# The last stage of a mixture-of-experts decoder step: a buffer for every tile, all gathers at once, no barrier, residuals put in PSUM ahead

## The chip, the cores and the metric

One core of a Trainium2 chip runs the whole step as one program. The metric is the device time of one execution in microseconds (us), lower is better. The core's engines each run their own instruction list: TensorE (PE in the rows, with PEld for its weight loads), VectorE (DVE), ScalarE (ACT), GpSimd (POOL) and SyncE (SP). They meet only at semaphores. Data moves between memory and the on-chip buffers by DMA, which SP, ACT and POOL issue.

## The reference

One step of a one-layer decoder: attention and a recurrent mixer, then a hierarchical mixture of experts, for 1024 prompt tokens and 32 sample tokens, all in float32. What matters here is the end of it:

```python
x = x + mixed @ w_out[l]                          # x1 in the kernel
for e in range(N_EXPERTS):
    he = jax.nn.silu(t @ w1[e]) * (t @ w3[e])
    y = y + combine[:, e:e + 1] * (he @ w2[e])
x = x + y                                         # two experts a token have combine > 0
y_prompt = rmsnorm(xp, final_norm_w)
```

Each token has two chosen experts with gates `gate1` and `gate2`. So the last stage computes, for a token, x1 + gate1 * ya + gate2 * yb, where ya and yb are the two experts' outputs for it, and then the root mean square norm of that row times `final_norm_w`.

## The kernel before

The kernel sorts the (token, expert) pairs by expert. An expert loop runs over blocks of 160 sorted rows, two blocks a turn (`s` = 0 and 1, `turns` + 1 turns). For a block TensorE flips the rows (L1947, L1949), computes the hidden layer (L1962) and the down projection (L1977 for 32 rows, L1982 for 128), ACT and DVE copy the halves of the result out of PSUM (L1910, L1912, L2057), and ACT stores them to `ye_d`, the expert scratch in memory (L1914, L1916). The last block's store is the last thing that the last stage needs, since a token's rows can be in any block.

The last stage runs over TILES = 9 tiles of tokens: eight of 128 rows and one of 32. `x1[i]` holds the residual rows of tile i on chip. `phase_end` (L450 to 453) is a barrier: each engine drains, increments one semaphore and waits until all five have. Behind it, for tile i:

- POOL gathers the two experts' rows from `ye_d` into `ya` and `yb` (L1895, one indirect DMA each). There are YBUF = 5 pairs of buffers. From tile 5 on POOL first waits for ACT's sum of squares of tile i - 5 and for the output store of that tile.
- TensorE puts the residual into two PSUM banks by a product with the identity (L2005; banks 2 * (i % 4) and the next, and from tile 4 on it waits for the combination of tile i - 4, by `x2_ready`), waits for the gather of `yb`, and adds the product of diag(gate2) with `yb` into the same banks (L2008). Each of these two is a group of two matmuls of 512 columns, each of which the rows count as two instructions, so x4. Below they are called the residual and the gated product.
- DVE combines, ya * gate1 + PSUM, in two halves (L2085, `combine`), and later takes the inverse root of tile i's mean square by five small instructions (L2019 and L2025 to L2028, `mean_eps` and `inverse`) and scales the row with `fw` (L2097, the result). Its order is combine(0), then for each i: combine(i + 1), the inverse root of i, the result of i.
- ACT sums the squares (L1931) and takes their root (L1934); ahead of the tiles it loads `fw` (L1927).
- SP stores the result (L1865).

The semaphore `mixed` tells DVE that a gated product is done, `x2_ready` tells ACT and TensorE that a combination is done, `ssf` and `rmsf` are ACT's, `y_ready` lets SP store. Every engine executes its list in order, and there is no planner: the order of the work is the order in which the lines stand.

Of the kernel before, what the change touches and what calls it, by code (L numbers as in the profile page):

```python
# [10 lines left out]
ALU = mybir.AluOpType  # L11
# [4 lines left out]
P = 128  # L16
D = 1024
# [107 lines left out]
def build(nc, x_prompt, x_sample, cache_k, cache_v, state_hgrn, page_table,  # L125
# [30 lines left out]
    with ExitStack() as ctx:  # L156
# [89 lines left out]
        YBUF = 5  # L246
        ya = [take(D, T0 + i * D) for i in range(YBUF)]
        yb = [take(D, T0 + (YBUF + i) * D) for i in range(YBUF)]
        fw = take(D, T0 + 2 * YBUF * D)
        diag2 = take(TILES * P, G0 + 64)  # L250

        tab = sb("tab", SMALL)
# [1594 lines left out]
        @block.sync  # L1847
        def _(sp):
            turns = sp.value_load(more_i[0:1, 0:1], min_val=1, max_val=PAIRS - 1)
            with sp.Fori(0, turns) as t:  # L1850
                for s in range(2):
                    e = sp.value_load(eid[0:1, ds(t * 2 + (s + 2), 1)], min_val=0, max_val=NE - 1)
                    w13 = wslot[s][:, 0:4096].rearrange("p (k f) -> p k f", k=KC)
                    sp.wait_ge(sem("h1_ps"), t * 2 + s + 1)
                    sp.dma_start(w13[:, :, 0:FF], w1_v[ds(e * D, D), :].rearrange("(k p) f -> p k f", p=P)).then_inc(sem(f"wexp{s}"), 16)
                    sp.wait_ge(sem("h_ps"), t * 2 + s + 3)
                    sp.dma_start(w13[:, :, FF:2 * FF], w3_v[ds(e * D, D), :].rearrange("(k p) f -> p k f", p=P)).then_inc(sem(f"wthr{s}"), 16)
                    sp.wait_ge(sem("ye_ps"), t * 6 + 3 * s + 9)
# [7 lines left out]
            for i in range(YBUF):  # L1866
                sp.wait_ge(sem(f"y_out{i}"), 16 * len(range(i, TILES, YBUF)))

        @block.gpsimd
        def _(pool):  # L1870
# [13 lines left out]
            with pool.Fori(0, turns) as t:  # L1884
                for s in range(2):
                    pool.wait_ge(sem("xgT_ps"), t * 2 + s + 1)
                    gather(t + 1, s)
            phase_end(pool, 1)

            for i in range(TILES):  # L1890
                if i >= YBUF:
                    pool.wait_ge(sem("ssf"), i - YBUF + 1)
                    pool.wait_ge(sem(f"y_out{i % YBUF}"), 16 * (i // YBUF))
                for c, buf in enumerate((ya, yb)):
                    pool.indirect_dma_start(out=buf[i % YBUF][0:ROWS[i], :], out_offset=None, in_=ye_d,  # L1895
                                            in_offset=bass.IndirectOffsetOnAxis(ap=slot_i[0:ROWS[i], c * TILES + i:c * TILES + i + 1], axis=0)).then_inc(sem(f"yg{c}{i % YBUF}"), 16)

        @block.scalar
        def _(act):
# [22 lines left out]
                    results(t, s)  # L1922
            act.wait_ge(sem("ye_out0"), nit * 32 + 32)
            act.wait_ge(sem("ye_out1"), nit * 32 + 32)
            act.sem_inc(sem("ye_seen"), 1)
            phase_end(act, 1)
            act.dma_start(fw, final_norm_w.rearrange("(a n) -> a n", a=1).broadcast_to([P, D])).then_inc(sem("fw"), 16)  # L1927
            for i in range(TILES):
                r = ROWS[i]
                act.wait_ge(sem("x2_ready"), i + 1)  # L1930
                nc.scalar.activation(yb[i % YBUF][0:r, :], ya[i % YBUF][0:r, :], ACT.Square,  # L1931
                                     accum_out=ss[0:r, i:i + 1]).then_inc(sem("ssf"), 1)
                act.wait_ge(sem("ssf"), i + 1)
                nc.scalar.activation(rstd[0:r, i:i + 1], ss[0:r, i:i + 1], ACT.Sqrt, scale=1.0 / D, bias=epsc[0:r, :]).then_inc(sem("rmsf"), 1)  # L1934

        @block.tensor
        def _(pe):
# [57 lines left out]
            with pe.Fori(0, turns) as t:  # L1995
                pair(t, True)
            pair(turns, False)
            phase_end(pe, 1)

            for i in range(TILES):  # L2000
                r = ROWS[i]
                if i >= 4:
                    pe.wait_ge(sem("x2_ready"), i - 3)
                for n in range(2):
                    nc.tensor.matmul(ps[2 * (i % 4) + n][0:r, :], ident[0:r, 0:r], x1[i][0:r, n * 512:(n + 1) * 512], start=True, stop=False)  # L2005
                pe.wait_ge(sem(f"yg1{i % YBUF}"), 16 * (i // YBUF + 1))
                for n in range(2):
                    mm = nc.tensor.matmul(ps[2 * (i % 4) + n][0:r, :], diag2[0:r, i * P:i * P + r], yb[i % YBUF][0:r, n * 512:(n + 1) * 512], start=False, stop=True)  # L2008
                mm.then_inc(sem("mixed"), 1)

        @block.vector
        def _(dve):
# [62 lines left out]
            dve.wait_ge(sem("fw"), 16)  # L2075

            ch2 = Chain(dve, sem("dve_last"))

            def combine(i):
                r = ROWS[i]  # L2080
                dve.wait_ge(sem(f"yg0{i % YBUF}"), 16 * (i // YBUF + 1))
                dve.wait_ge(sem("mixed"), i + 1)
                a_ = ya[i % YBUF][0:r, :]
                for n in range(2):
                    last = V.scalar_tensor_tensor(out=a_[:, n * 512:(n + 1) * 512], in0=a_[:, n * 512:(n + 1) * 512], scalar=gate1[0:r, i:i + 1],  # L2085
                                                  in1=ps[2 * (i % 4) + n][0:r, :], op0=ALU.mult, op1=ALU.add)
                last.then_inc(sem("x2_ready"), 1)

            combine(0)
            for i in range(TILES):  # L2090
                if i + 1 < TILES:
                    combine(i + 1)
                r = ROWS[i]
                dve.wait_ge(sem("rmsf"), i + 1)
                ch2.step(mean_eps(ss[0:r, i:i + 1], D))
                inverse(rstd[0:r, i:i + 1], ss[0:r, i:i + 1], ch2)
                V.scalar_tensor_tensor(out=ya[i % YBUF][0:r, :], in0=ya[i % YBUF][0:r, :], scalar=rstd[0:r, i:i + 1], in1=fw[0:r, :],  # L2097
                                       op0=ALU.mult, op1=ALU.mult).then_inc(sem("y_ready"), 1)


# [29 lines left out]
```

## Time and profile before

| | |
|---|---|
| three runs, median | 1472.09 us (1469.22 to 1472.66) |
| the profiled execution | 1467.2 us, span 1465.4 us |
| its mean granted TensorE clock | 0.94 of full speed |
| TensorE, DVE, ACT, POOL busy | 87%, 43%, 25%, 8% of the span |
| from the first gather to the end of the span | 1414.37 to 1465.4, 51 us |

The span is the profiled execution's time from its first to its last recorded event; the 1.8 us around it are start and end of the program. Times in rows are microseconds from the span's start.

### The profile page before, as it was taken

Reading aid. Unit: us, or ns where it says so; the run is one execution under the profiler, and the core shown is the slowest. Engines: PE = TensorE matmul, PEld = TensorE weight load, DVE = VectorE, ACT = ScalarE, POOL = GpSimd, SP = SyncE. Lnnn points to the kernel's source line nnn. Section 1 sums busy time; section 2 is a strip of 40 time slices with the busy share of each in tenths; the row PEclk is TensorE's granted clock in tenths of the full one; section 3 lists DMA queues with packets and bytes.
Section 4 is the critical chain, followed back from the end, with each engine's and each line's share of the span. In section 5 each row is a group of like instructions: output and inputs, shape, how many; then the busy total and the mean of one; then the engine's idle time right before and its main releaser. Section 6 shows DMA issues by size and latency. Waiting matters only on the chain. (4 is left out here: it accounts for less than half of the span.)

```text
span 1465.4 us, 24091 instructions
## 1 busy us (share of the span) xinstructions
PE 1268.1 (87%) x9162; PEld 894.7 (61%) x9162; DVE 633.4 (43%) x1518; ACT 372.8 (25%) x748; POOL 111.2 (8%) x272
## 2 busy tenths in 40 slices
PE   0899998989999899988787886999995299999976
PEld 0566785767678788655364553555553188888842
DVE  0401314445354646366866764467336212121117
ACT  3401200121212224244545552222212011111113
POOL 0500000000000001020000000000000111111022
PEclk9999998999999999999898988999997599999999
DMA  7521101010020106667786969999840679999746
GB/s 207 205 111 51 58 29 43 30 31 30 0 88 1 60 3 215 229 249 260 287 299 237 318 231 380 334 355 348 299 152 19 208 250 304 297 304 299 251 174 231
DMA packets 163717, 274.02 MB, mean 187 GB/s; under 512 B 19041, under 2 KB 78178, under 8 KB 163618
## 3 DMA queue, kind: packets, MB, share of 16 engines
q1 hardware_dynamic: 141072, 221.90, 44.6%
q0 software_dynamic: 11104, 38.28, 7.3%
q10 hardware_dynamic: 11442, 12.51, 2.7%
q8 instruction: 63, 1.03, 0.3%
q14 instruction: 36, 0.29, 0.1%
HBM read 235.55 MB, written 37.09 MB: 186 GB/s over the span
## 5 line engine op out<-in xcount | busy, mean ns | idle before, releaser
L973 PE MATMUL bank<-arena 128*128 128x352 f32 x768 | 237.6, 468 | 0.0
L973 PEld LDWEIGHTS bank<-arena 128*128 128x128 f32 x768 | 146.8, 194 | 80.2 <-issue 5.2
L976 PE MATMUL bank<-arena 128*128 128x256 f32 (+1 forms) x864 | 195.2, 383 | 0.6 <-issue 0.6
L976 PEld LDWEIGHTS bank<-arena 128*128 128x128 f32 (+1 forms) x864 | 155.0, 182 | 33.0 <-issue 5.7
L1546 DVE STREAM_TRANSPOSE arena<-arena 128x512 f32<-128x512 f32 x256 | 156.2, 677 | 21.4 <-DMA arena<-in_cache_k_dram 21.0
L1962 PEld LDWEIGHTS bank<-arena 128*128 128x128 f32 x1024 | 142.6, 192 | 9.2 <-issue 9.2
L1962 PE MATMUL bank<-arena 128*128 128x160 f32 x1024 | 143.7, 302 | 1.9 <-DVE arena L2047 1.9
L1250 PE MATMUL bank<-arena 128*128 128x512 f32 x256 | 119.7, 611 | 7.5 <-DMA arena<-in_w_out_dram 7.5
L1095 PE MATMUL bank<-arena,tab 128*32 128x256 f32 x1024 | 71.3, 426 | 19.8 <-ACT arena L779 13.1
L1250 PEld LDWEIGHTS bank<-arena 128*128 128x128 f32 x256 | 46.9, 193 | 60.8 <-issue 53.0
L719 ACT ACTIVATE arena<-bank 128x352 f32<-128x352 f32 x48 | 22.2, 463 | 224.5 <-PE bank L973 224.5
L1095 PEld LDWEIGHTS bank<-arena,tab 128*32 128x32 f32 x1024 | 33.7, 120 | 58.5 <-issue 27.3
L1136 PE MATMUL bank<-arena 128*32 128x128 f32 x2048 | 65.9, 275 | 0.1
L851 ACT ACTIVATE arena<-arena,small 128x128 f32<-128x128 f32 (+7 forms) x64 | 48.9, 765 | 63.5 <-DVE small L1610 63.5
L2052 DVE TENSOR_TENSOR arena<-arena,bank 128x320 f32<-128x320 f32 x16 | 7.8, 488 | 130.4 <-PE bank L1962 130.4
L1180 PE MATMUL bank<-arena 64*128 64x512 f32 (+3 forms) x192 | 58.7, 618 | 6.1 <-DVE small L1610 6.0
L1136 PEld LDWEIGHTS bank<-arena 128*32 128x32 f32 x2048 | 53.0, 110 | 16.5 <-issue 14.7
L1982 PE MATMUL bank<-arena 128*128 128x512 f32 x128 | 59.2, 605 | 0.0
L1016 PEld LDWEIGHTS bank<-arena 128*128 128x128 f32 x448 | 54.3, 192 | 4.4 <-issue 0.4
L1016 PE MATMUL bank<-arena 128*128 128x128 f32 x448 | 54.6, 275 | 0.0
L1472 DVE COPY_PREDICATED arena<-tab,bank 128x512 f32<-128x512 int32 x56 | 37.4, 721 | 36.0 <-PE bank L1020 36.0
L1202 PE MATMUL bank<-arena 128*128 128x128 f32 x288 | 46.5, 303 | 7.0 <-ACT arena L872 7.0
(306 smaller groups left out, 1474.6 us busy)
## 6 DMA issues: line engine op xcount, KB each, us to landing
arena<-in_cache_k_dram SPq DMA_DIRECT2D x256, 256.0 KB, 4.7
arena<-in_cache_v_dram SPq DMA_DIRECT2D x256, 256.0 KB, 3.9
arena<-in_expert_w_dram SPq DMA_DIRECT2D x48, 1024.0 KB, 8.6
arena<-in_w_in_dram SPq DMA_DIRECT2D x14, 1024.0 KB, 5.1
expert_scratch<-route POOLq DMA_DIRECT2D x40, 256.0 KB, 5.6
expert_scratch<-arena ACTq DMA_DIRECT2D x16, 512.0 KB
out_dram<-arena SPq DMA_DIRECT2D x12, 512.0 KB, 2.9
arena<-in_x_prompt_dram SPq DMA_DIRECT2D x4, 1024.0 KB, 10.9
```

Of the source, the lines that this page charges most:

```text
L851: nc.scalar.activation(zp[n % 2][:, sl], zp[n % 2][:, sl], ACT.Exp, scale=-1.0, bias=a[:, m:m + 1], accum_out=a[:, 2 + m:3 + m]).then_inc( ...
L973: mm = nc.tensor.matmul(bank(g)[:, 0:N3], w[:, k, c * P:(c + 1) * P], hT[:, k * TOK + n * N3:k * TOK + (n + 1) * N3], start=(k == 0), stop ...
L976: mm = nc.tensor.matmul(bank(g)[0:ROWS[c], 0:256], tok(hT, k, c), w[:, k, :], start=(k == 0), stop=(k == KC - 1))
L1016: mm = nc.tensor.matmul(ps[bb + c // 4][:, (c % 4) * P:(c % 4 + 1) * P], a, b_, start=True, stop=True)
L1095: mm = nc.tensor.matmul(ps[5][32 * h:32 * h + 32, 0:256], q[:, c * 32:(c + 1) * 32], k8[:, :, c, :], start=(j == 0), stop=(j == 3))
L1136: mm = nc.tensor.matmul(ps[7][32 * h:32 * h + 32, 0:P], lhs, ring4[q4 % QUADS][:, i * HW + h * P:i * HW + (h + 1) * P], start=(g == 0 and ...
L1180: nc.tensor.matmul(ps[k % 3][:, 0:w], qT[rows, h * TOK + i * P:h * TOK + (i + 1) * P], kT[rows, h * TOK + j * P:h * TOK + j * P + w], star ...
L1202: mm = nc.tensor.matmul(ps[4][:, 0:P], pT[k % PCH][:, (jj % 4) * P:(jj % 4 + 1) * P], v_nat[:, jj * HW + h * P:jj * HW + (h + 1) * P], sta ...
L1250: mm = nc.tensor.matmul(ps[n][:, :], tok(mix_da if kk < H else mix_hg, kk % H, i), wout[k][:, n * 512:(n + 1) * 512], start=(k == 0), stop ...
L1546: V.transpose(page, page).then_inc(sem("k_flip"), 1)
L1962: mm = nc.tensor.matmul(ps[3 + m // 2][:, (m % 2) * TR:(m % 2 + 1) * TR], w13[:, k, m * P:(m + 1) * P], xT[s][:, k * TR:(k + 1) * TR], sta ...
L1982: mm = nc.tensor.matmul(ps[5 + n][:, :], he[s][:, k * TR:k * TR + P], w2[:, k * D + n * 512:k * D + (n + 1) * 512], start=(k == 0), stop=( ...
```

## The change

`ya` and `yb` get nine buffers each; `yb` takes over the space of the experts' weights, `ya` and `fw` that of the expert loop's blocks. With that all waits of POOL inside the last stage go, and it issues its 18 gathers in one go, each pair counted on one semaphore for tile i. All five calls of `phase_end` go; POOL waits for the stores' own semaphores instead. TensorE puts the residuals of tiles 0 to 3 into the eight banks as soon as the expert loop has left them, and inside the loop over tiles the residual of tile i + 4 stands behind the gated product of tile i. ACT computes one Sqrt ahead of the tiles on a value that isn't used, and then takes one Sqrt for two tiles. DVE takes the inverse root for two tiles at a time, in an order with the results two tiles behind the combinations.

```diff
@@ sync
-            phase_end(sp, 1)
             for i in range(TILES):
                 sp.wait_ge(sem("y_ready"), i + 1)
                 dst = ys_v if i == TILES - 1 else yp_v[:, i, :]
-                sp.dma_start(dst, ya[i % YBUF][0:ROWS[i], :]).then_inc(sem(f"y_out{i % YBUF}"), 16)
+                sp.dma_start(dst, ya[i][0:ROWS[i], :]).then_inc(sem("y_out"), 16)
...
@@ gpsimd
-            phase_end(pool, 1)
-
+            pool.wait_ge(sem("ye_out0"), turns * 32 + 64)
+            pool.wait_ge(sem("ye_out1"), turns * 32 + 64)
+            pool.sem_inc(sem("ye_seen"), 1)
             for i in range(TILES):
-                if i >= YBUF:
-                    pool.wait_ge(sem("ssf"), i - YBUF + 1)
-                    pool.wait_ge(sem(f"y_out{i % YBUF}"), 16 * (i // YBUF))
                 for c, buf in enumerate((ya, yb)):
...
@@ scalar
-            act.sem_inc(sem("ye_seen"), 1)
-            phase_end(act, 1)
             act.dma_start(fw, final_norm_w.rearrange("(a n) -> a n", a=1).broadcast_to([P, D])).then_inc(sem("fw"), 16)
+            nc.scalar.activation(att[:, 0:1], epsc, ACT.Sqrt)
             for i in range(TILES):
                 r = ROWS[i]
                 act.wait_ge(sem("x2_ready"), i + 1)
...
+                nc.scalar.activation(yb[i][0:r, :], ya[i][0:r, :], ACT.Square, accum_out=ss[0:r, i:i + 1]).then_inc(sem("ssf"), 1)
+                if i % 2 or i == TILES - 1:
+                    j = i - i % 2
+                    act.wait_ge(sem("ssf"), i + 1)
+                    nc.scalar.activation(rstd[0:r, j:i + 1], ss[0:r, j:i + 1], ACT.Sqrt, scale=1.0 / D, bias=epsc[0:r, :]).then_inc(sem("rmsf"), 1)
@@ tensor
-            phase_end(pe, 1)
-
+            def residual(i):
+                r = ROWS[i]
+                for n in range(2):
+                    nc.tensor.matmul(ps[2 * (i % 4) + n][0:r, :], ident[0:r, 0:r], x1[i][0:r, n * 512:(n + 1) * 512], start=True, stop=False)
+
+            pe.wait_ge(sem("xT_s"), turns * 6 + 9)
+            residual(0)
+            pe.wait_ge(sem("ye_a"), turns * 4 + 6)
+            pe.wait_ge(sem("ye_v"), turns * 2 + 3)
+            residual(1)
+            residual(2)
+            residual(3)
             for i in range(TILES):
                 r = ROWS[i]
-                if i >= 4:
-                    pe.wait_ge(sem("x2_ready"), i - 3)
+                pe.wait_ge(sem(f"yg{i}"), 32)
                 for n in range(2):
-                    nc.tensor.matmul(ps[2 * (i % 4) + n][0:r, :], ident[0:r, 0:r], x1[i][0:r, n * 512:(n + 1) * 512], start=True, stop=False)
-                pe.wait_ge(sem(f"yg1{i % YBUF}"), 16 * (i // YBUF + 1))
-                for n in range(2):
-                    mm = nc.tensor.matmul(ps[2 * (i % 4) + n][0:r, :], diag2[0:r, i * P:i * P + r], yb[i % YBUF][0:r, n * 512:(n + 1) * 512], start=False, stop=True)
+                    mm = nc.tensor.matmul(ps[2 * (i % 4) + n][0:r, :], diag2[0:r, i * P:i * P + r], yb[i][0:r, n * 512:(n + 1) * 512], start=False, stop=True)
                 mm.then_inc(sem("mixed"), 1)
+                if i + 4 < TILES:
+                    pe.wait_ge(sem("x2_ready"), i + 1)
+                    residual(i + 4)
@@ vector
-            phase_end(dve, 1)
...
+            def scales(i):
+                r, j = ROWS[i], i - i % 2
+                dve.wait_ge(sem("rmsf"), j // 2 + 1)
+                ch2.step(mean_eps(ss[0:r, j:i + 1], D))
+                inverse(rstd[0:r, j:i + 1], ss[0:r, j:i + 1], ch2)
...
+            dve.wait_ge(sem("fw"), 16)
             combine(0)
...
+            combine(1)
+            for i in range(2, TILES):
+                combine(i)
+                if i % 2 == 0:
+                    scales(i - 1)
+                result(i - 2)
+            result(TILES - 2)
+            scales(TILES - 1)
+            result(TILES - 1)
```

## Rows read from the trace of the kernel before

**Rows 1.** Page, part 1: engine, busy us, share of the span, instructions.
```profile
PE 1268.1 (87%) x9162; PEld 894.7 (61%) x9162; DVE 633.4 (43%) x1518; ACT 372.8 (25%) x748; POOL 111.2 (8%) x272
```

**Rows 2.** Timeline, 1404 to 1416 us: start, duration, engine, line; idle time before, releaser.
```profile
1404.55 0.49 DVE L2052 TENSOR_TENSOR arena<-arena,bank 128x320 f32<-128x320 f32 x1 [7.91 <-PE bank L1962]
...
1405.28 1.07 PE L1977 MATMUL bank<-arena 128*32 128x256 f32 x16 [0.76 <-DVE arena L2052]
...
1406.28 3.70 PE L1982 MATMUL bank<-arena 128*128 128x512 f32 x8
...
1410.87 0.35 ACTq L1916 DMA_DIRECT2D expert_scratch<-arena  x1
...
1414.37 0.94 POOL L1895 DMA_INDIRECT arena<-expert_scratch,route  x1 [49.49 <-ACTq L452]
...
1415.61 0.94 POOL L1895 DMA_INDIRECT arena<-expert_scratch,route  x1 [0.31 <-issue]
```

**Rows 3.** Chain that ended last, two pieces: start, us, what.
```profile
1410.87 3.12 DMA expert_scratch<-arena
...
1415.61 6.00 DMA arena<-expert_scratch,route
```

**Rows 4.** Timeline, tiles 0 to 3, 1421 to 1436 us.
```profile
1421.65 3.44 PE L2008 MATMUL bank<-arena 128*128 128x512 f32 x4 [3.92 <-DMA arena<-expert_scratch,route]
...
1425.24 1.41 DVE L2085 SCALAR_TENSOR_TENSOR arena<-arena,route,bank 128x512 f32<-128x512 f32 x2 [14.54 <-PE bank L2008]
...
1426.65 1.88 PE L2008 MATMUL bank<-arena 128*128 128x512 f32 x4
...
1426.68 1.06 ACT L1931 ACTIVATE arena<-arena 128x1024 f32<-128x1024 f32 x1 [17.79 <-DVE arena L2085]
...
1427.85 1.28 ACT L1934 ACT_TABLE_LOAD   x1
...
1428.64 1.41 DVE L2085 SCALAR_TENSOR_TENSOR arena<-arena,route,bank 128x512 f32<-128x512 f32 x2 [1.99 <-PE bank L2008]
...
1432.08 1.41 DVE L2085 SCALAR_TENSOR_TENSOR arena<-arena,route,bank 128x512 f32<-128x512 f32 x2
...
1434.24 1.28 DVE L2097 SCALAR_TENSOR_TENSOR arena<-arena,small 128x1024 f32<-128x1024 f32 x1
```

**Rows 5.** Timeline, TensorE at tiles 5 and 6, 1442 to 1450 us.
```profile
1442.68 1.98 PE L2008 MATMUL bank<-arena 128*128 128x512 f32 x4 [2.13 <-DMA arena<-expert_scratch,route]
...
1444.50 1.88 PE L2005 MATMUL bank<-arena,tab 128*128 128x512 f32 x4
...
1448.04 1.98 PE L2008 MATMUL bank<-arena 128*128 128x512 f32 x4 [1.66 <-DMA arena<-expert_scratch,route]
```

**Rows 6.** Waits, 1400 to 1466 us: total us, times, longest.
```profile
DVE arena L2085 <- PE bank L2008: 21.2, 5, 14.5
POOL arena L1895 <- DMA out_dram<-arena: 17.1, 4, 9.1
```

**Rows 7.** Timeline, tile 8's combination and the last result.
```profile
1457.48 1.39 DVE L2085 SCALAR_TENSOR_TENSOR arena<-arena,route,bank 32x512 f32<-32x512 f32 x2
...
1461.61 1.27 DVE L2097 SCALAR_TENSOR_TENSOR arena<-arena,small 32x1024 f32<-32x1024 f32 x1
```

**Rows 8.** The gathers' line, L1895: time from issue to landing.
```profile
DMA to landing us min/median/max: 6.0/6.7/7.8
```

**Rows 9.** DMA queues, 1380 to 1466 us: POOL's queue, packets, MB, share.
```profile
q0 software_dynamic: 2400, 8.65, 27.4%
```

**Rows 10.** Windows: length; busy PE, PEld, DVE, ACT, POOL; granted clock, DMA share, GB/s.
```profile
650.00:651.00 1.00, 1.00 (x4) 0.55 (x4) 0.34 (x2) 0.97 (x4) 0.77 (x4) 0.50 1.01 406
...
1422.00:1423.00 1.00, 1.00 (x2) 0.48 (x2) 0.00 (x0) 0.00 (x0) 0.76 (x1) 0.50 1.02 414
...
1441.00:1442.00 1.00, 0.00 (x0) 0.00 (x0) 0.96 (x2) 0.83 (x3) 0.18 (x1) 1.00 1.04 426
```

**Rows 11.** Timeline, TensorE around 649 us.
```profile
649.50 0.33 PE L1192 MATMUL bank<-tab,arena 128*128 128x128 f32 x1 [1.05 <-DVE arena L1622]
```

More of the change, by code:

```diff
@@ L244, in build @@
         ysb, ysm = [take(D, M0[s] + 2624) for s in range(2)], [take(256, M0[s] + 3648) for s in range(2)]
[L246 to L249, printed above, removed]
+        ya = [take(D, T0 + i * D) for i in range(TILES)]
+        yb = [take(D, C0 + i * D) for i in range(TILES)]
+        fw = take(D, T0 + TILES * D)
         diag2 = take(TILES * P, G0 + 64)
@@ L1864, in _ @@
                 dst = ys_v if i == TILES - 1 else yp_v[:, i, :]
-                sp.dma_start(dst, ya[i % YBUF][0:ROWS[i], :]).then_inc(sem(f"y_out{i % YBUF}"), 16)
-            for i in range(YBUF):
-                sp.wait_ge(sem(f"y_out{i}"), 16 * len(range(i, TILES, YBUF)))
+                sp.dma_start(dst, ya[i][0:ROWS[i], :]).then_inc(sem("y_out"), 16)
+            sp.wait_ge(sem("y_out"), 16 * TILES)
         @block.gpsimd
@@ L1887, in _ @@
                     gather(t + 1, s)
-            phase_end(pool, 1)
+            pool.wait_ge(sem("ye_out0"), turns * 32 + 64)
+            pool.wait_ge(sem("ye_out1"), turns * 32 + 64)
+            pool.sem_inc(sem("ye_seen"), 1)
             for i in range(TILES):
-                if i >= YBUF:
-                    pool.wait_ge(sem("ssf"), i - YBUF + 1)
-                    pool.wait_ge(sem(f"y_out{i % YBUF}"), 16 * (i // YBUF))
                 for c, buf in enumerate((ya, yb)):
-                    pool.indirect_dma_start(out=buf[i % YBUF][0:ROWS[i], :], out_offset=None, in_=ye_d,
-                                            in_offset=bass.IndirectOffsetOnAxis(ap=slot_i[0:ROWS[i], c * TILES + i:c * TILES + i + 1], axis=0)).then_inc(sem(f"yg{c}{i % YBUF}"), 16)
+                    pool.indirect_dma_start(out=buf[i][0:ROWS[i], :], out_offset=None, in_=ye_d,
+                                            in_offset=bass.IndirectOffsetOnAxis(ap=slot_i[0:ROWS[i], c * TILES + i:c * TILES + i + 1], axis=0)).then_inc(sem(f"yg{i}"), 16)
         @block.scalar
@@ L1930, in _ @@
                 act.wait_ge(sem("x2_ready"), i + 1)
[L1931 to L1934, printed above, removed]
+                nc.scalar.activation(yb[i][0:r, :], ya[i][0:r, :], ACT.Square, accum_out=ss[0:r, i:i + 1]).then_inc(sem("ssf"), 1)
[3 more added lines that the diff above has]
+                    nc.scalar.activation(rstd[0:r, j:i + 1], ss[0:r, j:i + 1], ACT.Sqrt, scale=1.0 / D, bias=epsc[0:r, :]).then_inc(sem("rmsf"), 1)
         @block.tensor
@@ L2071, in _ @@
             pair(turns, False)
-            phase_end(dve, 1)
-            dve.wait_ge(sem("fw"), 16)
             ch2 = Chain(dve, sem("dve_last"))
@@ L2080, in combine, with result @@
                 r = ROWS[i]
-                dve.wait_ge(sem(f"yg0{i % YBUF}"), 16 * (i // YBUF + 1))
                 dve.wait_ge(sem("mixed"), i + 1)
-                a_ = ya[i % YBUF][0:r, :]
                 for n in range(2):
-                    last = V.scalar_tensor_tensor(out=a_[:, n * 512:(n + 1) * 512], in0=a_[:, n * 512:(n + 1) * 512], scalar=gate1[0:r, i:i + 1],
+                    last = V.scalar_tensor_tensor(out=ya[i][0:r, n * 512:(n + 1) * 512], in0=ya[i][0:r, n * 512:(n + 1) * 512], scalar=gate1[0:r, i:i + 1],
                                                   in1=ps[2 * (i % 4) + n][0:r, :], op0=ALU.mult, op1=ALU.add)
                 last.then_inc(sem("x2_ready"), 1)
-            combine(0)
[L2090 to L2098, printed above, removed]
+            def scales(i):
[3 more added lines that the diff above has]
+                inverse(rstd[0:r, j:i + 1], ss[0:r, j:i + 1], ch2)
+            def result(i):
+                r = ROWS[i]
+                V.scalar_tensor_tensor(out=ya[i][0:r, :], in0=ya[i][0:r, :], scalar=rstd[0:r, i:i + 1], in1=fw[0:r, :],
+                                       op0=ALU.mult, op1=ALU.mult).then_inc(sem("y_ready"), 1)
+            dve.wait_ge(sem("fw"), 16)
+            combine(0)
+            combine(1)
[7 more added lines that the diff above has]
+            result(TILES - 1)
 _INS = ['x_prompt', 'x_sample', 'cache_k', 'cache_v', 'state_hgrn', 'page_table', 'norm1_w', 'w_in', 'rel_bias',
```

## The prediction

> **What bounds the kernel now.** The page comes first: TensorE is busy 87% of the span [rows 1]. That average is made by the stages ahead; the change touches only what comes after the last expert, so I read the timeline and the chain from 1405 us on. There the last down-projection ends at 1409.98, and ACT's store of its result is issued at 1410.87 and lands at 1413.99. Only then can a row be gathered: POOL's first gather starts at 1414.37, tile 0's second at 1415.61. That one takes 6.0 us to land, and TensorE starts tile 0's gated product at 1421.65 [rows 2 to 4]. The last stage proper is thus 1421.65 to 1465.4, 43.8 us.
>
> Inside it each tile needs 1.72 us of TensorE for the residual product and 1.72 for the gated one (TensorE works there without a gap, two groups every 3.43 us; a single group's own span, with its drain, is 1.88), and on DVE 1.41 for the combination, about 0.75 for the inverse root (from the end of the combination, 1433.49, to the result's start at 1434.24) and 1.27 for the result. Both sums are 3.43 to 3.44 us, and combinations do follow each other so: 1428.64, 1432.08 [rows 4]. So in its free running part TensorE and DVE are equal bounds, because the residual of tile i+1 runs while DVE combines tile i. From tile 5 on the gathers come late: POOL waits 17.1 us in four waits for output stores that free its five buffers, and TensorE starts tiles 5 and 6 late, after pauses of 2.13 and 1.66 us [rows 5, 6]. DVE's five waits are 21.2 us, of which 14.5 lie ahead of tile 0 and 1.99 ahead of tile 1 [rows 4, 6]. The other three make 4.7 us: that is all that the buffers cost at the end of the path. After tile 8's combination (1457.48 + 1.39) the results of tiles 7 and 8 end at 1462.88, and the end of the span, 1465.4, is 2.5 us later [rows 7].
>
> **The change, part by part.**
>
> *Barrier.* The first gather starts 0.38 us after the store landed (1413.99 to 1414.37). POOL also needs 0.31 between two gathers without any barrier [rows 2, 3]. So the removal is worth 0 to 0.4 us; I take 0.1, since a wait, a semaphore and the same preparation stay ahead of the gather.
>
> *Buffers and gathers.* 18 gathers at 1.24 us each [rows 2] start from 1414.3 to 1435.4 and, with landings of 6.0 to 7.8 us [rows 8], are in by 1443.2. The bytes don't forbid it: 8.65 MB for the gathers and 0.5 MB for the norm weights, at the 414 GB/s of a busy stretch, take 22 us; an output store of 0.5 MB adds 1.3 us [rows 9, 10]. The pairs are ready well before the times that I find below, so no gather is late any more: the 4.7 us go. Late next is then whatever orders TensorE and DVE.
>
> *Residuals ahead.* Four residual groups run on TensorE from 1410 to about 1417 (four times 1.72), in time in which it waits anyway [rows 2, 4]. In the kernel before, tile 0's residual hid behind its gather too, and the others beside DVE. Gain 0 as long as DVE keeps up; what follows from their order is more. But all eight banks are then full, and tile i+4's residual needs the banks of tile i. TensorE works in program order, and the new order is: gated product i, wait for the combination of i, residual i+4, gated product i+1. Behind the new wait stands the gated product of the next tile, though its rows have landed and its banks are ready; DVE waits for that. What were two engines side by side becomes one loop:
> gated product's start to DVE's start 1.99 (1426.65 to 1428.64, DVE idle before) + combination 1.41 + DVE's end to TensorE's start 0.24 (1405.04 to 1405.28) + residual after a wait until the next group 1.82 (1442.68 to 1444.50) = 5.46 us a tile [rows 2, 4, 5]. The hand-over from DVE is the least sure term. From below it can be DVE's to ACT, 0.03 (1426.65 to 1426.68), which makes 5.25; above it, I keep 0.3, for 5.5. I take 0.24, which is the same pair of engines.
> The Trainium skill, "TensorE: Matmul & The Clock Gate", section Step-by-step: what each phase is for, says that only weight loads are pulled ahead and matmuls stay in program order. No row here shows a matmul overtaking one that waits. If one could, the loop would not exist, and the sum would be that of the first rival.
>
> *The sum.* Tile 0's combination starts at 1425.24 - 0.1 = 1425.14. Residuals 4 to 8 follow combinations 0 to 4, so the loop runs five times: tile 5's combination starts at 1425.14 + 5 x 5.46 = 1452.44. DVE keeps up meanwhile: its longest work between two combinations is 0.75 + 1.27 = 2.02, and it has 5.46 - 1.41 = 4.05. From there on no residual is left (tiles 6 to 8 follow at 1.72) and DVE is the bound. Its list from the combination of 5 on is 4 combinations, 6 results (3 to 8) and 3 inverse roots (for 4-5, 6-7, 8): 5.64 + 7.62 + 2.25 = 15.5 us. The last result ends at 1467.95; with the same 2.5 us of store and end [rows 7] the span is 1470.5 against 1465.4: +5.1 us.
>
> *Where that stands against the kernel before.* The loop costs 5 x (5.46 - 3.43) = 10.1. DVE's lists from tile 0 on differ by four inverse roots (3.0 saved), but most of the saving falls into DVE's idle time inside the loop. The results are kept back by one tile more, so after the last combination there stand an extra result (1.27), while 4.7 of stalls are gone.
>
> *Small parts.* ACT's table load (1.28 us, at 1427.85) moves ahead of tile 0 into idle time; before, it ended at 1429.13, covered by the combination of tile 1 until 1430.05 [rows 4]; without that cover it would have cost its 1.28 once. Gain 0. Sums of squares (1.06 + 0.19) and half as many Sqrts lie beside DVE work; one pair follows 1.6 us after its combination, while DVE has a combination or result to do: 0, at most 1.27 if DVE were out of work. SP's stores have no queue ahead of them.
>
> **Against the runs.** The profiled run took 1467.2 us, 1.8 over its span; the runs' median, 1472.09, is 4.9 above it. The change is in the last 50 us, so I add the difference to both: 1472.3 in the form of that profiled run, and 1477.2 us against the median.
>
> **The rivals.**
>
> *No loop: DVE alone is the bound.* If residual i+4 didn't hold back the gated product (say, because the next group was let through), DVE would run through: 9 x 1.41 + 9 x 1.27 + 5 x 0.75 = 27.9 from 1425.14, end 1453.0 + 2.5 = 1455.5, so -9.9 us: 1462.2. For it: DVE's waits would be gone with the late gathers. Against it: the order of the waits in the code, and TensorE's program order. Its point of decision is whether DVE's work between two combinations exceeds 4.05 us; it is 2.02.
>
> *The first group runs at the full clock.* The clock is a second term in tile 0. TensorE had paused 3.9 us before 1421.65 and its gated product took 3.44 us at granted clock 0.50 (the 1.2 GHz level); the same group at 1426.65 took 1.88 at 2.4 GHz, and the pauses of 2.13 and 1.66 us later did not lower the clock [rows 4, 5, 10]. After the change the pause is about 4.6 us (1417 to 1421.6), so I expect the same low start. If it stays high instead, 3.44 becomes 1.88 and all moves 1.6 us earlier: +3.5, 1475.6, which counts as no change.
>
> *The loop lowers the clock.* This is the side beyond the forecast. In the loop TensorE works 3.7 us and pauses 1.76. Rows for: at 649.50 it had paused 1.05 us amid smaller products, and in the microsecond from 650 on the clock was 0.50 [rows 10, 11]. Rows against: with pauses of that size and the very same products the groups at 1442.68 and 1448.04 took 1.98, full clock [rows 5, 10]. One stretch of low clock costs about what it cost for tile 0, 1.6 us; two of them make +8.3, 1480.4; if it stayed low, each of ten groups would cost 1.56 more, +20.7, 1493.
> The Trainium skill's page on TensorE, section A second HAM failure mode: psum-queue depth-cycling, describes just this: short idle times between groups that cycle through banks make the clock swing. By it this rival would be the rule; the trace of this stage doesn't show it, so it keeps a small chance.
>
> *The change does little.* If the order were right but the hand-overs shorter (5.25 a tile), the sum is +4.0; with a store or landing saved at the end it drops to +2 or 3: no change by measurement.
>
> **How the numbers follow.** A measurement of this kernel can tell about 0.3% (4.4 us) from no change. Chances: forecast loop at full clock 0.55, with its own range +3.4 to +6.5 (1475.5 to 1478.6), of which I put 0.13 under 4.4 us; low clock in the loop 0.15; full clock at the first group 0.12; little change by shorter terms 0.08; no loop, faster 0.10. So faster 0.10, same 0.33, slower 0.57. The likeliest is the forecast, 1477.2. For the range I leave out the fast rival (0.10) and the far end of the low clock: 1471.5 to 1484, which also takes in a couple of microseconds by which medians of such runs differ (1469.2 to 1472.7 before).
>
> **What would show it.** Right: combinations of tiles 0 to 5 start some 5.4 us apart, DVE and TensorE both idle inside each; TensorE's residual waits for DVE's combination line; all gathers start 1.24 us apart and none is waited for after tile 0; from tile 5 on DVE has no idle time for 15.5 us. Wrong: combinations 3 us apart from the start (no loop), a granted clock of 0.5 after 1428, or gathers that land more than 20 us after their start.

## The result, and the profile after

The median of 22 runs after is 1476.51 us (lowest 1471.89, highest 1481.06) against 1470.64 us (1464.51 to 1477.19) of 22 runs of the kernel before beside it. The ratio is 1.0039 with a 95% interval of 1.0028 to 1.0050: slower by 5.9 us, where +5.1 was forecast. The profiled execution took 1474.43 us, span 1472.6, which is 7.2 us above the span before; the forecast span was 1470.5.

The page's engine line answers [rows 1]; nothing can be read from it alone, the change lies in 50 us of 1470.

```profile
PE 1269.7 (86%) x9162; PEld 894.1 (61%) x9162; DVE 630.1 (43%) x1498; ACT 371.7 (25%) x745; POOL 111.3 (8%) x272
```

The chain that ended last, from the last expert's store on (start, us, what), answers [rows 3]:

```profile
1410.96 3.13 DMA expert_scratch<-arena
1414.12 0.79 issue
1414.91 0.94 POOL arena L1890
1415.85 0.30 issue
1416.16 5.40 DMA arena<-expert_scratch,route
1421.56 0.04 issue
1421.60 3.80 PE bank L2009 x4
1425.44 0.06 issue
1425.50 1.42 DVE arena L2082 x2
1426.92 0.04 issue
1426.96 3.78 PE bank L1996 x4
1430.74 1.90 PE bank L2009 x4
1432.67 1.42 DVE arena L2082 x2
1434.09 0.04 issue
1434.13 1.98 PE bank L1996 x4
1436.12 1.73 PE bank L2009 x4
1437.87 1.42 DVE arena L2082 x2
...
1449.73 1.97 PE bank L1996 x4
1451.70 3.51 PE bank L2009 x4
1455.23 1.40 DVE arena L2082 x2
```

L2082 is the combination, L1996 the residual product, L2009 the gated one. The chain is the predicted loop: combination, residual, gated product, combination, with TensorE waiting for each combination and each combination for TensorE. Combinations start at 1425.50, 1432.67, 1437.87, 1443.07, 1448.27 and 1455.23: three steps of 5.20 us, and one of 7.17 and one of 6.96 at the ends.

The timeline of TensorE over the same stretch (start, duration, line, idle time before and its releaser) answers [rows 4, 5]. It shows both what was expected, the pauses of 1.5 us for DVE, and what wasn't: the residual at 1426.96 takes 3.78, and the gated product after the small residual of tile 8 (32 rows) is slow too: 3.51 in the chain above. The last row puts it together with the three products behind it.

```profile
1421.60 3.78 PE L2009 MATMUL bank<-arena 128*128 128x512 f32 x4 [4.67 <-DMA arena<-expert_scratch,route]
1426.96 3.78 PE L1996 MATMUL bank<-arena,tab 128*128 128x512 f32 x4 [1.58 <-DVE arena L2082]
1430.54 2.10 PE L2009 MATMUL bank<-arena 128*128 128x512 f32 x4
1434.13 1.98 PE L1996 MATMUL bank<-arena,tab 128*128 128x512 f32 x4 [1.50 <-DVE arena L2082]
1435.95 1.88 PE L2009 MATMUL bank<-arena 128*128 128x512 f32 x4
...
1449.73 1.97 PE L1996 MATMUL bank<-arena,tab 32*32 32x512 f32 x4 [1.50 <-DVE arena L2082]
...
1451.63 8.83 PE L2009 MATMUL bank<-arena 128*128 128x512 f32 x16
```

The windows (length; busy PE, PEld, DVE, ACT, POOL; granted clock, DMA share, GB/s) say why: the granted clock is 0.50, the 1.2 GHz level, in both places, and 1.00 between. They answer [rows 10].

```profile
1428.00:1429.00 1.00, 1.00 (x3) 0.48 (x2) 0.00 (x0) 0.09 (x1) 0.69 (x2) 0.50 1.12 406
1436.00:1437.00 1.00, 1.00 (x4) 0.52 (x3) 0.00 (x0) 0.00 (x0) 0.82 (x1) 1.00 0.99 406
1453.00:1454.00 1.00, 1.00 (x2) 0.34 (x1) 0.00 (x0) 0.00 (x0) 0.00 (x0) 0.50 0.84 344
```

The waits from 1400 us on (total us, times, longest) answer [rows 6]. POOL has no wait for output stores left, so the late gathers are gone; DVE's waits for the gated product grew from 21.2 to 32.1, and TensorE has a new one for the combination, 7.6 us in five.

```profile
DVE arena L2082 <- PE bank L2009: 32.1, 6, 14.7
PE bank L1996 <- DVE arena L2082: 7.6, 5, 1.6
POOL arena L1890 <- issue: 5.2, 17, 0.3
```

The gathers' line answers [rows 8]: no slower than before.

```profile
DMA to landing us min/median/max: 5.2/5.6/7.8
```

DVE's last result, from the timeline, answers [rows 7]; it ends 2.4 us ahead of the end of the span.

```profile
1468.97 1.27 DVE L2094 SCALAR_TENSOR_TENSOR arena<-arena,small 32x1024 f32<-32x1024 f32 x1
```

### The profile page after: what moved, and what is told of

It is laid out like the page before. It is cut to its first block and busy times, and to the rows that moved or that the text cites. A ratio compares the mean times of both kernels' runs of the same rounds, so it can differ in the third digit from the quotient of the medians.

```text
span 1472.6 us, 24051 instructions
## 1 busy us (share of the span) xinstructions
PE 1269.7 (86%) x9162; PEld 894.1 (61%) x9162; DVE 630.1 (43%) x1498; ACT 371.7 (25%) x745; POOL 111.3 (8%) x272
## 5 line engine op out<-in xcount | busy, mean ns | idle before, releaser
L1545 DVE STREAM_TRANSPOSE arena<-arena 128x512 f32<-128x512 f32 x256 | 156.2, 676 | 21.2 <-DMA arena<-in_cache_k_dram 20.8
L1249 PEld LDWEIGHTS bank<-arena 128*128 128x128 f32 x256 | 47.1, 194 | 62.9 <-issue 53.5
L1015 PE MATMUL bank<-arena 128*128 128x128 f32 x448 | 54.6, 275 | 0.0
```

What stands on the lines that cost most here:

```text
L1015: mm = nc.tensor.matmul(ps[bb + c // 4][:, (c % 4) * P:(c % 4 + 1) * P], a, b_, start=True, stop=True)
L1249: mm = nc.tensor.matmul(ps[n][:, :], tok(mix_da if kk < H else mix_hg, kk % H, i), wout[k][:, n * 512:(n + 1) * 512], start=(k == 0), stop ...
L1545: V.transpose(page, page).then_inc(sem("k_flip"), 1)
```

## The experiments

Ratios are against the kernel before on the same chip, with 95% intervals. As the whole time carries noise of other stages, each profile is also read by the length of its last stage: from the landing of the last expert's store to the end of the span. It is 51.4 us before (1413.99 to 1465.4) and 58.5 after (1414.09 to 1472.6). Each kernel has one profile, of one of its runs, so differences of stages under about 1 us are not told from chance: the landing of the rows and the length of the low clock alone differ by that much from profile to profile.

**1. The residual one gated product later.** All of the change is kept; only the place of the residuals 4 to 8 moves, so that the next gated product stands ahead of the wait.

```diff
-                if i + 4 < TILES:
-                    pe.wait_ge(sem("x2_ready"), i + 1)
-                    residual(i + 4)
+                if i >= 1 and i + 3 < TILES:
+                    pe.wait_ge(sem("x2_ready"), i)
+                    residual(i + 3)
```

> The changed kernel with one edit: residual i+3 behind gated product i (for i = 1 to 5) in place of residual i+4 behind gated product i, so that the wait for a combination stands one tile later. Same work, same buffers, same banks. Theory (the loop): TensorE no longer waits for the combination that it has only just fed; it needs two groups or 3.43 us a tile while residuals last, DVE needs 3.06, so combinations 2 to 5 follow 3.4 to 3.5 us apart instead of 5.20, DVE is without a pause from tile 5 on, and the last result ends about 12 us earlier: span about 1460, 5 us under the kernel before, 12 under the changed one. Rival (late rows or DVE's order are what costs): combinations stay over 5 us apart and the span stays within 2 us of the changed kernel's.

Measured: 1467.34 us, ratio 0.9966 (0.9941 to 0.9990); stage 47.1 us, 11.4 less than after, where 12 were expected. TensorE runs without a pause:

```profile
1424.16 6.61 PE L2009 MATMUL bank<-arena 128*128 128x512 f32 x8 [5.38 <-DMA arena<-expert_scratch,route]
1430.61 1.88 PE L1996 MATMUL bank<-arena,tab 128*128 128x512 f32 x4
1432.33 1.88 PE L2009 MATMUL bank<-arena 128*128 128x512 f32 x4
1434.04 1.88 PE L1996 MATMUL bank<-arena,tab 128*128 128x512 f32 x4
1435.76 1.88 PE L2009 MATMUL bank<-arena 128*128 128x512 f32 x4
```

and combinations follow at 1430.81, 1434.24, 1437.68: 3.43 to 3.44 us again. From tile 0's to tile 5's combination it takes 16.7 us instead of 29.7 (1428.06 to 1444.76, against 1425.50 to 1455.23). One position in TensorE's program makes the change a loss or a gain; the loop, with 3.7 us of low clock on top of its five steps (see below), is its cause.

**2. No residual ahead.** Each residual stands right ahead of its own gated product, as before, and the one behind the gated product goes; buffers and gathers are those of the change. Only residual 0 is still early.

```diff
-            residual(1)
-            residual(2)
-            residual(3)
             for i in range(TILES):
+                if i >= 4:
+                    pe.wait_ge(sem("x2_ready"), i - 3)
+                if i:
+                    residual(i)
```

> The changed kernel with the residual order of the kernel before: residual 0 early, every other residual right ahead of its own gated product, no residual put in banks ahead. Nine buffers, no barrier, DVE and ACT as changed. Theory (the loop): TensorE and DVE run side by side again, tiles 3.43 us apart, last result about 1460, span about 1462.5: 10 us under the changed kernel and 3 under the kernel before, so putting residuals ahead is worth about nothing and its order costs all of the loss. Rival (putting residuals ahead helps, something else costs): this is as slow as the changed kernel or slower.

Measured: 1465.94 us, 0.9961 (0.9941 to 0.9982); stage 48.1, 10.4 less than after, where 10 were expected. Within the measurement this equals experiment 1: by the profiles residuals ahead gain 1.0 us, by the medians they lose 1.4, so no gain of theirs is shown.

**3. The buffers alone**, in the kernel before.

```diff
-        YBUF = 5
+        YBUF = TILES
...
-        yb = [take(D, T0 + (YBUF + i) * D) for i in range(YBUF)]
-        fw = take(D, T0 + 2 * YBUF * D)
+        yb = [take(D, C0 + i * D) for i in range(YBUF)]
+        fw = take(D, T0 + YBUF * D)
```

> The kernel before with nine pairs of buffers instead of five and nothing else: barriers, order of TensorE, DVE and ACT as before. Theory: all 18 gathers start 1.24 us apart, the three late DVE waits of 4.7 us go and nothing else changes: span about 1460.7, 0.3% under the kernel before. Rival (the stores or landings become late in their place, since gathers and stores now share the DMA engines at the same time): less than 2 us gained, with DVE waits for a late gather after tile 3.

Measured: 1467.81 us, 0.9979 (0.9959 to 1.0000), so 3.2 us less in the medians; in the profile the stage is 50.0, only 1.4 less, where 4.7 was the term. The waits for late gathers are gone: from tile 4's combination to tile 8's it takes 13.4 us instead of 18.5. But most of that came back ahead of them: tile 1's combination follows tile 0's after 4.63 us instead of 3.40, as the low clock of tile 0 lasts into the next residual (3.15 us at 1426.83), and DVE stands before the combinations of tiles 2 and 3 (2.2 us together) for reasons that TensorE doesn't give. The chain of waits at the longer of the two:

```profile
1439.33 1.45 another core or an unknown queue
```

**4. The barrier put back** into the changed kernel, one line on each engine, ACT's signal with it.

```diff
             pool.sem_inc(sem("ye_seen"), 1)
+            phase_end(pool, 1)
...
             act.wait_ge(sem("ye_out1"), nit * 32 + 32)
+            act.sem_inc(sem("ye_seen"), 1)
+            phase_end(act, 1)
```

> The changed kernel with the five calls of the barrier put back in their places, so residual 0 to 3 start only at the barrier too. In the changed kernel the first gather started 0.79 us after the last store had landed, in the kernel before 0.38. Theory (the barrier cost nothing, its removal gained nothing): first gather 0.3 to 0.4 us after the landing, residuals from 1414.2 to 1421, so TensorE has no pause of 4.7 us ahead of tile 0, and its clock may be high there; span within 2 us of the changed kernel's, lower if the clock is high at tile 0 (up to 4). Rival (removal of the barrier saves what it seemed to cost): span 0.4 us or more longer than the changed kernel's, with the same clock at tile 0.

Measured: 1478.73 us, 1.0037 (1.0014 to 1.0060), no different from the change's own 1.0039, so the barrier's absence is no gain that shows; stage 59.5. The 0.3 to 0.4 us expected was a miss: POOL's own end of phase, which now stood behind its wait for the store instead of ahead of it, took 2.68 us, and the first gather started 3.55 us after the landing. The chain of waits shows it, and with it an accident that is of use: TensorE was held at the barrier too and then ran into tile 0's product without a pause.

```profile
1418.63 2.68 POOLq L451
1421.31 0.04 issue
1421.35 9.51 PE bank L2000 x16
1430.87 1.72 PE bank L2014 x4
```

The first loop step then took 5.20 us (1432.73 to 1437.93) instead of 7.17. The last one, behind the residual of tile 8, again took 7.01.

**5. TensorE busy ahead of tile 0.** Two groups more, whose results nobody uses, between the residuals of tiles 2 and 3 of the changed kernel.

```diff
             residual(2)
+            for f in range(2):
+                for n in range(2):
+                    nc.tensor.matmul(ps[6 + n][:, :], ident, x1[0][:, n * 512:(n + 1) * 512], start=True, stop=True)
             residual(3)
```

> The changed kernel with two more groups of identity products into the banks of tile 3, ahead of that tile's residual, whose start clears them: 3.4 us of work whose result isn't used, put into TensorE's pause ahead of tile 0 (1416.9 to 1421.6 in the changed kernel's trace). Theory (part of the loss is the low clock that follows this pause): TensorE is busy until about 1420.4, the granted clock stays 1.00, the gated product of tile 0 takes 1.88 instead of 3.78 us and the first step of the loop 5.20 instead of 7.17, so everything from there is about 3.9 us earlier; from the last store's landing to the end of the span 54.6 us instead of 58.5. Rival (the clock in this stage depends on something else, as the pauses of the loop): gated product 0 still takes over 3 us, or the first step still over 7.

Measured: 1475.43 us, 1.0027 (1.0009 to 1.0044); stage 56.1, 2.4 less than after. In TensorE's timeline the pause ahead of tile 0 fell from 4.67 to 1.36 us, and the clock is high from the first product on, up to tile 8's residual (the step behind that took 6.96 us).

```profile
1421.87 1.98 PE L2012 MATMUL bank<-arena 128*128 128x512 f32 x4 [1.36 <-DMA arena<-expert_scratch,route]
1425.44 1.98 PE L1996 MATMUL bank<-arena,tab 128*128 128x512 f32 x4 [1.58 <-DVE arena L2085]
```

So the low clock at tile 0 goes with the long pause. The stage was expected at 54.6; 1.28 of the difference is tile 2's combination, which started late (1435.66, a step of 6.48) though its product was ready.

**6. Both: the order of experiment 1 and the two extra groups of experiment 5.**

> The residuals one tile later (as in e1_order) and the two groups of unused products in the pause ahead of tile 0 (as in e5_busy_ahead). Theory: both gains add, because without the loop DVE is the bound from tile 0's combination on, and that comes 1.9 us earlier: landing of the last store to the end of the span 44 us (47.1 in e1_order, 58.5 in the changed kernel, 51.4 in the kernel before), so about 0.5% under the kernel before in time. Rival (the gathers become the bound: a pair lands each 2.5 us and stores share the DMA engines): combinations wait for rows and the stage stays at 46 us or more.

Measured: 1469.15 us, 0.9985 (0.9969 to 1.0001); stage 51.8 where 44 was expected. Up to tile 2 it ran as it should. Then DVE stood still, and from 1441.66 TensorE behind it. DVE's combinations of tiles 2 and 3, and TensorE's product of tile 3:

```profile
1434.83 1.41 DVE L2085 SCALAR_TENSOR_TENSOR arena<-arena,route,bank 128x512 f32<-128x512 f32 x2 [2.17 <-issue]
1444.84 1.40 DVE L2085 SCALAR_TENSOR_TENSOR arena<-arena,route,bank 128x512 f32<-128x512 f32 x2 [6.51 <-DMA arena<-in_w_out_dram]
...
1436.34 1.88 PE L2012 MATMUL bank<-arena 128*128 128x512 f32 x4
```

The product was done at 1438.22, DVE's result of tile 0 at 1438.33, and the first output store was issued at 1438.36. The combination of tile 3, which needs nothing else that the program names, started 6.51 us later. The releaser named there is a transfer of the first stages; it is no cause. POOL went on issuing its last gathers meanwhile, up to 1441.47.

**7. Tile 8's residual over all 128 rows** in the changed kernel, 96 of them unused.

```diff
             def residual(i):
-                r = ROWS[i]
+                r = P
```

> The changed kernel with tile 8's residual computed for 128 rows and columns instead of 32 (the rows above 32 aren't used). In the changed kernel's trace and in e4_barrier_back the clock fell to 0.50 right behind that small group, and tile 5's combination came 7.0 us after tile 4's instead of 5.20. Theory (small products let the clock fall, not the loop's pauses of 1.5 us): with a full group the clock stays 1.00 there and the step is 5.20: the stage is 1.8 us shorter. Rival (the pauses do it, whatever the size of the group): the step stays near 7.0, or the low clock turns up in another step.

Measured: the last loop step took 5.20 us (combinations at 1450.85 and 1456.05) instead of 6.96, with the clock high, as expected:

```profile
1454.00:1455.00 1.00, 1.00 (x4) 0.39 (x3) 0.31 (x1) 0.00 (x0) 0.00 (x0) 1.00 0.00 0
```

The time shows no gain (1481.24 us, 1.0064, 1.0041 to 1.0088). The profile, with a stage of 57.2, 1.3 less than after, is of the fastest of its five runs (1475.25; the others lie from 1480.76 to 1481.95), and no profile shows what the slower ones spend. So the effect on the clock is seen in one profile, and why the median lies above that of after is open.

**8. ACT gives the sign for the first gather** (on top of experiment 6).

```diff
-            pool.wait_ge(sem("ye_out0"), turns * 32 + 64)
-            pool.wait_ge(sem("ye_out1"), turns * 32 + 64)
-            pool.sem_inc(sem("ye_seen"), 1)
+            pool.wait_ge(sem("ye_seen"), 1)
...
             act.wait_ge(sem("ye_out1"), nit * 32 + 32)
+            act.sem_inc(sem("ye_seen"), 1)
```

> e6_order_busy with one other edit: POOL waits on one semaphore that ACT increments behind its own waits for the stores, instead of waiting for the two stores' semaphores by a register's value and incrementing one itself. With the barrier (kernel before, e3) the first gather started 0.36 to 0.38 us behind the landing, without it (changed kernel, e1, e2) 0.79 to 0.82. Theory (the form of POOL's wait costs it, not the absence of the barrier): first gather 0.4 us behind the landing, and all behind it 0.4 us earlier. Rival (the barrier warmed POOL up, for example by fetching its next instructions): still 0.8.

Measured: 1469.59 us, 0.9986 (0.9966 to 1.0006); stage 52.1. The first gather started 0.29 us after the landing (1414.44 to 1414.73) instead of 0.82: right. The stall came again at the same place, 6.85 us ahead of tile 3's combination, from the moment of the first output store (issued at 1433.39). Two windows inside it, with TensorE, DVE, ACT and POOL all idle and the DMA engines full, and the chain:

```profile
1437.00:1438.00 1.00, 0.00 (x0) 0.00 (x0) 0.00 (x0) 0.00 (x0) 0.00 (x0) 1.00 0.99 406
1438.00:1439.00 1.00, 0.00 (x0) 0.00 (x0) 0.00 (x0) 0.00 (x0) 0.00 (x0) 1.00 1.04 426
```

```profile
1433.37 6.82 another core or an unknown queue
1440.19 0.02 issue
1440.21 1.42 DVE arena L2084 x2
```

It ended as the traffic of the gathers and of the first store did (332 GB/s in 1439 to 1440, 135 in the next). No packet of the instruction queues falls in it, and POOL had issued its last gather by 1436.62, so neither late instructions nor work that the profile shows on POOL explain it. It cost more than itself: after its pause of 5.00 us TensorE ran the next residual at the low clock (3.78 us at 1441.67). Two remedies were tried, each on top of this kernel: keep the stores away from the gathers, or the gathers away from the stores.

**9. Output stores only when the last gathers have landed.**

```diff
+            sp.wait_ge(sem("yg8"), 32)
             for i in range(TILES):
                 sp.wait_ge(sem("y_ready"), i + 1)
```

> e8_act_signal with one edit: SP waits until the last pair of rows has landed before it stores its first result, so no store shares the DMA engines with the gathers. In e6_order_busy and e8_act_signal DVE stood still for 6.5 and 6.9 us at tile 3's combination, from the moment at which the first store was issued until the gathers' traffic ended, although tile 3's gated product had started seven microseconds earlier; this ate what the earlier start had gained. Theory S (a store among the saturated gathers causes the stall): the stall is gone, combinations follow at 3.4 us, and the stage from the last landing to the end is 5 to 6 us shorter than e8's 52.1, about 46.5. Rival T (the gathers alone do it): DVE still stands for over 3 us somewhere between 19 and 27 us after the landing of the last expert's store, and the stage stays near 52.

Measured: 1463.12 us, 0.9954 (0.9937 to 0.9971); stage 44.9. No stall:

```profile
1430.35 1.41 DVE L2085 SCALAR_TENSOR_TENSOR arena<-arena,route,bank 128x512 f32<-128x512 f32 x2 [2.49 <-PE bank L2012]
...
1433.78 1.41 DVE L2085 SCALAR_TENSOR_TENSOR arena<-arena,route,bank 128x512 f32<-128x512 f32 x2
```

**10. Gathers in step with the combinations**: those of tile 4 wait for tile 0, and so on.

```diff
             for i in range(TILES):
+                if i >= 4:
+                    pool.wait_ge(sem("x2_ready"), i - 3)
```

> e8_act_signal with one edit: POOL issues the pairs of tiles 4 to 8 each only when the combination of four tiles before is done, so the gathers are no longer all in one go and the DMA engines' queues are shorter from tile 4 on. No pair is needed earlier than it can land. Theory T (all gathers in one go fill the DMA queues, and TensorE or DVE stand still until they empty): the stall of 6.9 us in e8_act_signal becomes less than 2, the stage 5 us or more shorter than its 52.1. Rival (the stall has nothing to do with how many gathers are outstanding): still over 5 us between 19 and 27 us after the landing.

Measured: 1464.19 us, 0.9949 (0.9936 to 0.9962); stage 44.8, no stall, combinations 3.43 apart in the middle (1435.56, 1438.99, 1442.42). Here stores and gathers do overlap (first store issued at 1439.05, last gather at 1445.3), with fewer gathers outstanding.

**11. DVE's order of before**, one inverse root a tile (ACT's root too) and each result one tile behind, in the kernel of experiment 1.

```diff
             combine(0)
-            combine(1)
-            for i in range(2, TILES):
-                combine(i)
-                if i % 2 == 0:
-                    scales(i - 1)
-                result(i - 2)
+            for i in range(TILES):
+                if i + 1 < TILES:
+                    combine(i + 1)
+                scales(i)
+                result(i)
```

> e1_order (residuals one tile later) with DVE's and ACT's order of the kernel before: an inverse root for every tile, results one tile behind the combinations. The prediction's working says: four inverse roots more (3.0 us of DVE work), but a result less behind the last combination; from e1_order's tile 0 on 8 tiles of 3.43 us, then 1.4 + 4.0 + 2.5, so the stage is 47.4 us against e1_order's 47.1: the pairing is worth nothing while TensorE also needs 3.43 us a tile. Rival (paired roots are a gain of their own): the stage is 2 us or more longer than e1_order's.

Measured: 1464.2 us, 0.9962 (0.9947 to 0.9976); stage 45.4, where 47.4 was expected, against 47.1 of experiment 1. Of the 1.7 us some 0.9 is a shorter stretch of low clock (tile 0 and 1's products in 5.71 us instead of 6.61), and 0.6 is tile 0's rows, which landed in 5.52 us instead of 6.10. From there on the two kernels differ by 0.3. So the paired inverse roots of the change are no gain that shows; nor is a loss shown.

This run bears on the stall too. Its first store was issued with the gathers in flow (393, 410 and 418 GB/s in the microseconds from 1433 on), and DVE did not stand: combinations follow at 1433.05, 1436.48, 1439.92 and 1443.35.

```profile
1433.09 7.20 SPq L1863 DMA_DIRECT2D out_dram<-arena  x3
```

## Why the prediction was right, point by point

*What is late next.* The step that decided: freeing POOL's buffers takes away a stall, and behind it stands the order in TensorE's program. The chain of after shows that loop, and experiments 1 and 2 take it away by order alone: -11.4 and -10.4 us of stage. The rival without a loop (1462.2 us, 9.9 under the kernel before) is out for the kernel as changed. Its sum also leaves out that TensorE then is a bound, with 3.43 us a tile while residuals last: without the loop the stage was 4.3 us under that of before (experiment 1), and with the clock and the stall mended too 6.5 (experiments 9 and 10), not 9.9.

*Length of a step.* 5.46 was predicted, 5.20 measured: 1.92 from product to DVE, 1.42, 0.04, and 1.82 for the residual. The term that was mis-sized is the hand-over from DVE, taken as 0.24 from a row of other instructions; it measured 0.04. The start of the product to DVE's start, taken as 1.99, gave the other 0.07. The end that was put at 5.25 was nearer. Five steps come to 1.3 us less.

*The clock in the loop.* Rated at 0.15, it came partly true: a granted clock of 0.50 after 1428, which the prediction named as a sign of being wrong, is there twice. Its two stretches are just what "two of them" named, but not for the reason given: the pauses of 1.5 us didn't lower the clock in three steps out of five. The Trainium skill, "TensorE: Matmul & The Clock Gate", section A second HAM failure mode: psum-queue depth-cycling, has short idle times between groups make the clock swing; for full groups this trace doesn't agree, with 1.00 granted in 1436 to 1437 and groups of 1.88 to 1.98. What the runs tie it to is the long pause ahead of tile 0, whose low stretch now also holds residual 4 (7.17 - 5.20 = 1.97 us; experiments 4 and 5: 5.20), and the 32-row residual between two pauses of 1.5 (6.96 - 5.20 = 1.76; experiment 7: 5.20). Together 3.7 us that the forecast's case held at nothing. In the kernel before, the low stretch ended with tile 0's product [rows 4].

*The sum.* Tile 0's combination came 0.36 us later than forecast (its product took 3.78 at the low clock instead of 3.44), the five steps 1.3 less and 3.7 more, DVE's list from there 15.0 instead of 15.5, and the end 2.4 instead of 2.5: +2.1, which is 1472.6 against 1470.5. Misses of unlike sign made the time look better met than the terms are; that part is luck.

*Barrier and first gather.* Taken as a gain of 0.1 us; the gather came 0.82 after the landing instead of 0.38, so 0.44 was lost. Experiment 8 shows that the waits that replaced the barrier on POOL cost it: with ACT's signal it is 0.29. Whether it is the form of the waits, their number or POOL's increment behind them was not separated. The landing took 5.40 instead of 6.00 and hid the loss.

*Buffers.* -4.7 was the sum of three waits. Alone they gave 1.4 us in a profile and 3.2 in the medians, whose interval reaches no change. The 4.7 did go, but the step that failed is to book them at the end of the path unabridged: a longer stretch at the low clock (1.2 us from tile 0 to tile 1) and short stands of DVE while the DMA engines are full (2.2) took their place.

*Residuals ahead, table load.* Nothing that shows, as said: experiments 1 and 2 differ by 1.0 us of stage one way and 1.4 us of median the other, and the table load is off the chain.

*What stays open.* Why DVE stands up to 6.85 us in experiments 6 and 8. It was seen only with gathers in full flow, and went when stores waited (9) or gathers were paced (10). The Trainium skill, "Perfetto Trace Analysis", section DMA Instruction — HWDGE (DVE, Sync), says that DVE's and Sync's sequencers share one block that makes descriptors; whether a store of Sync's that is held up there could hold DVE, which issues no DMA in this kernel, no run here shows; experiment 9 would fit. But 1.28 us of such a stand in experiment 5 came ahead of any store (the first was issued at 1439.15), and experiments 1 and 11 had their first store (1437.74, 1433.09) amid full traffic without such a stand. So neither the mechanism is shown, nor that there is only one, nor that it would come in every run. In the changed kernel the loop is so slow that all rows are in (DMA share 0.02 in 1441 to 1442) when the first store is issued.

## What to carry to other kernels

An engine works in program order: a product issued ahead for tile i+4 that waits for tile i must stand behind the work of tile i+1 that is already ready, or two engines side by side become one loop. Ask of each stall you remove what is next in order, and of each pause you leave how long TensorE idles in it. "Everything issued at once" is not free: with the order mended, the kernels that started tile 0 earliest lost their gain to a stall (6 and 8) until output stores or gathers were kept back (9 and 10, 7.5 and 6.5 us under the kernel before). Nor is it always dear: experiment 11 keeps nothing back, has no products that nobody uses, and is 6.5 under too.

## What the runs showed of the hardware that was not expected

- A group of matmuls over 32 rows, between pauses of 1.5 us that full groups stood without loss, was followed by granted clock 0.50 (6.96 us for a step of 5.20, twice more at 7.01 and 6.96 in experiments 4 and 5); over 128 rows, in one profile, it was not.
- With POOL's waits on two DMA semaphores against a value in a register ahead of an indirect gather, it was 0.82 us from landing to issue; with one wait for a constant set by ACT 0.29. An end of phase on POOL behind such waits took 2.68 (experiment 4).
- DVE's end to TensorE's start was 0.04 us in each step of the loop, where 0.24 was read in the expert loop.
- With the DMA engines full (406 to 426 GB/s), a ready DVE instruction stood for 1.3 to 6.9 us in four kernels (experiments 3, 5, 6, 8); under the same traffic it did not in experiment 11.
- POOL's issue of a gather took 1.6 to 1.9 us instead of 0.94 now and then (experiments 1, 3, 10 and 11); no row tells why.
